# Layer norm without gain and bias in the stored rows: they come in with the turned copies and with GpSimd's residual rows

## The reference, cut to what matters

```python
def layer_norm(x, g, b):
    mu = mean(x); var = mean((x - mu) ** 2)
    return (x - mu) * rsqrt(var + 1e-5) * g + b

h = layer_norm(ALPHA * h + pool_mixer(h), ln_mix_g, ln_mix_b)     # ALPHA = 2 ** 0.25
gate, up = split(h @ w_gu)
f = (silu(gate) * up) @ w_down
out = layer_norm(ALPHA * h + f, ln_ffn_g, ln_ffn_b)
```

## Time and profile before

| | us |
|---|---|
| median of 3 runs | 1692.83 (1691.8 to 1693.13) |
| the profiled execution's own time | 1694.09 |
| its span, first to last instruction | 1692.3 |
| PE busy | 1660.9 (98%) |
| DVE busy | 977.0 (58%) |
| POOL busy | 608.9 (36%) |
| ACT busy | 582.9 (34%) |

### The profile page before, as it was taken

How to read it: one execution, slowest core, us unless ns; L and a number is a source line. 1 busy time by engine, 2 the same in 40 slices (tenths; PEclk the granted TensorE clock), 3 DMA queues, 4 the chain that set the end, 5 groups by cost and what they waited for, 6 DMA issues and landing times.

```text
span 1692.3 us, 19004 instructions
## 1 busy us (share of the span) xinstructions
PE 1660.9 (98%) x7400; PEld 1373.2 (81%) x7400; DVE 977.0 (58%) x1056; ACT 582.9 (34%) x790; POOL 608.9 (36%) x413
## 2 busy tenths in 40 slices
PE   7999999999999999999979999999999999999998
PEld 5888888788888888888868888888888888878886
DVE  6648677788744444444646554454554443558766
ACT  5322334244333333333533333333333332432220
POOL 0000015104445656465547666566532000341002
PEclk9999999999999999999999999999999999999999
DMA  8533647654354555465555555554659444554542
GB/s 316 207 125 128 242 143 282 244 211 168 114 173 156 187 193 193 143 223 173 185 172 181 162 159 163 173 152 137 196 143 336 151 135 155 191 196 174 197 156 92
DMA packets 182265, 305.66 MB, mean 181 GB/s; under 512 B 7584, under 2 KB 131616, under 8 KB 172448
## 3 DMA queue, kind: packets, MB, share of 16 engines
q1 hardware_dynamic: 142480, 272.46, 47.4%
q10 hardware_dynamic: 37520, 23.60, 4.6%
q0 software_dynamic: 2176, 8.39, 1.4%
HBM read 216.86 MB, written 87.56 MB: 180 GB/s over the span
## 4 chain that ended last, share of the span: by engine, by line
PE 92%; DVE 3%; DMA 3%; issue 1%; ACT 1%; SPq 0%; POOLq 0%; POOL 0%; DVEq 0%; ACTq 0%
PE acc L985 42%; PE acc L1014 18%; PE acc L831 9%; PE acc L847 9%; PE turn L985 7%; PE turn L1014 6%; PE turn L819 1%; DMA af_dram<-g 1%; DVE split L1342 1%; DMA z<-x 1%; DMA fold_dram<-fold_st 1%; DMA nat<-x_t 0%; DMA z<-w_group_t 0%; PE acc L892 0%; DVE sums L1375 0%
## 5 line engine op out<-in xcount | busy, mean ns | idle before, releaser
L985 PE MATMUL acc<-fb,wf 128*128 128x512 f32 x1584 | 364.5, 390 | 9.2 <-DVE g L1611 9.2
L985 PE MATMUL acc<-fa,wf 128*128 128x512 f32 x1584 | 366.1, 390 | 0.0
L985 PEld LDWEIGHTS acc<-fb,wf 128*128 128x128 f32 x1584 | 298.2, 188 | 71.7 <-issue 9.5
L985 PEld LDWEIGHTS acc<-fa,wf 128*128 128x128 f32 x1584 | 296.1, 188 | 61.2
L1014 PE MATMUL acc<-dw,da 128*128 128x512 f32 x1386 | 315.9, 389 | 0.7 <-DVE dw L1551 0.7
L1014 PEld LDWEIGHTS acc<-dw,da 128*128 128x128 f32 x1386 | 260.0, 188 | 55.5 <-DVE dw L1551 1.6
L1482 DVE TENSOR_TENSOR wf<-wt,wf 128x512 fp32r<-128x512 f32 x132 | 125.3, 950 | 180.8 <-ACT wf L1156 180.6
L1482 DVE TENSOR_TENSOR wf<-wr,wf 128x512 fp32r<-128x512 f32 x176 | 176.2, 1009 | 82.6 <-ACT wf L1156 82.1
L1156 ACT CAST wf<-wr 128x512 fp32r<-128x512 f32 x176 | 109.0, 620 | 236.1 <-PE acc L985 220.3
L681 POOL TENSOR_TENSOR wt<-wr,wt 128x512 f32<-128x512 f32 x88 | 129.4, 1471 | 147.4 <-DVE wf L1482 147.1
L847 PE MATMUL acc<-split,act_sb 128*128 128x512 f32 x768 | 176.7, 390 | 2.3 <-DVE split L1342 2.3
(11 more groups left out here) (108 smaller groups left out, 1634.3 us busy)
## 6 DMA issues: line engine op xcount, KB each, us to landing
wr<-w_gu SPq DMA_DIRECT2D x44, 1024.0 KB, 4.9
dar<-af_dram SPq DMA_DIRECT2D x56, 704.0 KB, 4.3
af_dram<-g ACTq DMA_DIRECT2D x33, 512.0 KB, 3.8
raw<-w_in SPq DMA_DIRECT2D x16, 1024.0 KB, 6.2
raw<-fold_dram SPq DMA_DIRECT2D x16, 1024.0 KB, 5.8
fs<-hf_dram SPq DMA_DIRECT2D x14, 1024.0 KB, 6.0
dt_raw<-w_down SPq DMA_DIRECT2D x22, 512.0 KB, 6.4
wt_dram<-dt_t SPq DMA_DIRECT2D x22, 512.0 KB, 3.8
```

Of the source, the lines that this page charges most:

```text
L985: mm = nc.tensor.matmul(dst, wf[:, slot, a, k, :], fa[half][i][:, v, :, k, :], start=i < 2 and k == 0 and n3 == 0, stop=k == KC - 1 and n3 ...
```

## The change

- `apply` and its two DVE passes over each of 16 tiles are gone. POOL's `rstd_of` also makes mean * rstd and its negative, `shift` (two operations on 128x4), and a new ACT operation `norm` makes z * rstd + shift in one pass over a tile. Stored and turned rows are then normalized, without g and b.
- `take_turn` multiplies by g and adds b, which now lie one value per partition (`mix_g_sb`, `mix_b_sb`): two ACT operations of 128x256 in place of one copy of 128x512.
- The residual rows in the down stage get ALPHA*g and ALPHA*b from POOL: two operations of 128x1024 for each of 16 tiles (32 in all). ALPHA is multiplied into a broadcast pair `mgb` by one ACT operation of 128x2048; ACT's 16 multiplications by ALPHA are gone. `mgb` is loaded when the last unit's first product is done. SP issues it behind the activations of step 2 and ahead of the residual rows.
- `take(k)` of t = 0 now waits for the row with gain (`hz_ready`), not for its landing.
- Five buffers `hs` in place of two; the first five tiles are loaded at k = 14 to 18.
- The early broadcast load of g and b (two of 512 KB) is replaced by two of 4 KB.

The core of the diff:

```diff
             def rstd_of(s):
                 pool.wait_ge(var_ready, s + 1)
+                if s:
+                    pool.wait_ge(normed, s * TT)
                 nc.gpsimd.tensor_tensor(rstd[:, 0:TT], var_eps[:, 0:TT], minus_half[:], ALU.pow).then_inc(rstd_ready, 1)
+                pool.wait_ge(rstd_ready, s + 1)
+                nc.gpsimd.tensor_tensor(mean_rstd[:], mv[:, 0:TT, 0], rstd[:, 0:TT], ALU.mult).then_inc(mean_scaled, 1)
+                pool.wait_ge(mean_scaled, s + 1)
+                sub(shift[:], zeros[:], mean_rstd[:]).then_inc(shift_ready, 1)
...
+            def rows_times_gain(rows, gained, ready, m):
+                nc.gpsimd.tensor_tensor(rows, rows, mgb[:, 0, :], ALU.mult).then_inc(gained, 1)
+                pool.wait_ge(gained, m + 1)
+                nc.gpsimd.tensor_tensor(rows, rows, mgb[:, 1, :], ALU.add).then_inc(ready, 1)
...
+            pool.wait_ge(mgb_scaled, 1)
+            for m in range(MT):
+                pool.wait_ge(hz_landed[m], 16)
+                rows_times_gain(z0[:, m].rearrange("p h t -> p (h t)"), hz_gained, hz_ready, m)
+            for m in range(len(hs)):
+                hs_times_gain(m)
             for m in range(MT):
                 pool.wait_ge(taken, taken_by(3, m))
-                pool.wait_ge(h12_scaled, m + 1)
+                pool.wait_ge(hz_ready, m + 1)
                 nc.gpsimd.tensor_tensor(z0[:, m, 1, :], z0[:, m, 1, :], z1[:, m, 1, :], ALU.add).then_inc(h12_added, 1)
-                pool.wait_ge(h2_scaled, m + 1)
+                pool.wait_ge(hs_ready, m + 1)
                 pool.wait_ge(h12_added, m + 1)
                 zz = z1[:, m].rearrange("p h t -> p (h t)")
-                nc.gpsimd.tensor_tensor(zz, zz, hs[:, m % 2], ALU.add).then_inc(h2_added, 1)
+                nc.gpsimd.tensor_tensor(zz, zz, hs[m % len(hs)][:], ALU.add).then_inc(h2_added, 1)
+                if m + len(hs) < MT:
+                    pool.wait_ge(h2_added, m + 1)
+                    hs_times_gain(m + len(hs))
...
-                nc.scalar.copy(st_of(pi)[:, :, k, :], turn[:, slot, :].rearrange("p (b t) -> p b t", t=P)
-                               ).then_inc(turn_taken, 1)
+                for n, kk in enumerate((k, KC + k)):
+                    nc.scalar.activation(st_of(pi)[:, 2 * n:2 * n + 2, k, :],
+                                         turn[:, slot, 2 * n * P:2 * (n + 1) * P].rearrange("p (b t) -> p b t", t=P),
+                                         ACT.Identity, bias=mix_b_sb[:, kk:kk + 1], scale=mix_g_sb[:, kk:kk + 1]
+                                         ).then_inc(turn_taken, 1)
...
+            def norm(s, j):
+                if j == 0:
+                    act.wait_ge(shift_ready, s + 1)
+                nc.scalar.activation(z[:, j, :], z[:, j, :], ACT.Identity, bias=shift[:, j:j + 1],
+                                     scale=rstd[:, j:j + 1]).then_inc(normed, 1)
...
             store_a(2 * JF - 1)
+            act.wait_ge(mgb_landed, 32)
+            nc.scalar.mul(mgb[:], mgb[:], ALPHA).then_inc(mgb_scaled, 1)
             for k in range(DSTEPS):
...
-                if t == 1:
-                    act.wait_ge(hz_landed[m], 16)
-                    nc.scalar.mul(z0[:, m, 1, :], z0[:, m, 1, :], ALPHA).then_inc(h12_scaled, 1)
-                if t == 3:
-                    act.wait_ge(hs_landed[m % 2], 16 * (m // 2 + 1))
-                    nc.scalar.mul(hs[:, m % 2], hs[:, m % 2], ALPHA).then_inc(h2_scaled, 1)
...
                 if t == 0:
-                    dve.wait_ge(hz_landed[m], 16)
-                    nc.vector.scalar_tensor_tensor(out=z0[:, m, 0, :], in0=z0[:, m, 0, :], scalar=ALPHA, in1=down_bank(k),
-                                                   op0=ALU.mult, op1=ALU.add).then_inc(taken, 1)
+                    dve.wait_ge(hz_ready, m + 1)
+                    nc.vector.tensor_tensor(z0[:, m, 0, :], z0[:, m, 0, :], down_bank(k), ALU.add).then_inc(taken, 1)
```

More of the change, by code:

```diff
@@ L131, in trunk @@
         dar = at("dar", V0, [P, 2, JF, P])
-        hs = at("hs", Z0, [P, 2, D])
+        hs = [at(f"hs{n}", off, [P, D]) for n, off in enumerate((Z0, Z0 + 4 * KB, G0, G0 + 4 * KB, G0 + 8 * KB))]
+        mgb = at("mgb", Z0 + 8 * KB, [P, 2, D])
         ident = sb("ident", [P, P])
         scale_sb = sb("scale_sb", [P, KT])
+        mix_g_sb = sb("mix_g_sb", [P, KT])
+        mix_b_sb = sb("mix_b_sb", [P, KT])
+        zeros = sb("zeros", [P, TT])
+        mean_rstd = sb("mean_rstd", [P, TT])
+        shift = sb("shift", [P, TT])
         stats = sb("stats", [P, 2 * MT, HALVES, 6])
@@ L169, in trunk @@
         hz_landed = [sem(f"hz_landed{m}") for m in range(MT)]
-        hs_landed = [sem("hs_landed0"), sem("hs_landed1")]
+        hs_landed = [sem(f"hs_landed{n}") for n in range(len(hs))]
+        mix_gb_landed = sem("mix_gb_landed")
+        mgb_landed = sem("mgb_landed")
         out_stored = sem("out_stored")
@@ L205, in trunk @@
         rstd_ready = sem("rstd_ready")
+        zeros_ready = sem("zeros_ready")
+        mean_scaled = sem("mean_scaled")
+        shift_ready = sem("shift_ready")
+        normed = sem("normed")
+        mgb_scaled = sem("mgb_scaled")
+        hz_gained = sem("hz_gained")
+        hz_ready = sem("hz_ready")
+        hs_gained = sem("hs_gained")
+        hs_ready = sem("hs_ready")
         centered = sem("centered")
@@ L519, in _ @@
             load_chunk(c_in(0, 1), 1, w_in[1])
-            for n, v in enumerate((mix_g, mix_b)):
-                sp.dma_start(gb[:, n, :], v.partition_broadcast(P)).then_inc(gb_landed, 16)
+            for tile, v in ((mix_g_sb, mix_gt), (mix_b_sb, mix_bt)):
+                sp.dma_start(tile[:], v).then_inc(mix_gb_landed, 16)
             load_chunk(c_in(0, 2), 0, w_in[2])
@@ L663, in _ @@
                         load_dw(t + 1, q)
[L664 to L667, removed]
+                if 14 <= k < 14 + len(hs):
+                    load_hs(k - 14)
+                if t == 3 and 3 <= m < 3 + MT - len(hs):
+                    load_hs(m - 3 + len(hs))
                 if t == 4 and 2 <= m < 2 + LATE:
@@ L1174, in mixer_block @@
                         take_turn(i - 1, 1)
+                    if b:
+                        for j in ((0, 1), (2,), (3,), ())[i]:
+                            norm(b - 1, j)
                     if b == LAST and i >= 2:
@@ L1274, in _ @@
                 nc.scalar.copy(s5[:], bank_d).then_inc(s5_taken, 1)
+                if n in (1, 2):
+                    norm(LAST, 2 * (n - 1))
+                    norm(LAST, 2 * (n - 1) + 1)
                 if turned_in(n)[0] is not None:
@@ L1407, in aggregate @@
             def aggregate(s):
+                if s:
+                    dve.wait_ge(normed, s * TT)
                 for j in range(TT):
@@ L1504, in mixer_block @@
                         d_lo(b, i - 1)
-                    if not first:
-                        for j in ((0, 1), (), (2,), (3,))[i]:
-                            apply(b - 1, j)
                     if b == LAST and i >= 2:
@@ L1591, in _ @@
                     up_out(jj, 0, bank(n, 0))
-                if n in (1, 2):
-                    apply(LAST, 2 * (n - 1))
                 if nxt:
@@ L1622, in _ @@
                     act_form_lo(1)
-                if n in (1, 2):
-                    apply(LAST, 2 * (n - 1) + 1)
                 if nxt:
```

61 lines of the change are left out of this document (32 added, 29 removed).

## The result

The median of the changed kernel is 1707.01 us (1704.1 to 1707.62, 4 runs), that of the kernel before in the same rounds 1692.93 us (1691.8 to 1693.13, 4 runs). The ratio is 1.0081 with a 95% interval of 1.0068 to 1.0093: slower by 14.1 us, where 14.6 were forecast. The profiled execution took 1707.62 us, its span is 1705.8 us at a mean granted clock of 0.992, 13.5 us over the span before. Of the later runs two single executions, 1860.45 us (run 6) and 6585.92 us (run 11), lie far outside all others, and no ratio counts them.

The account below looks back on a forecast made before the run. PE, busy 98% of the span with 31.4 us idle, was taken as the bound. Terms 0.4 + 10.2 + 4.0 = 14.6 us, added to the median 1692.83, gave 1707.4 us; range 1693 to 1717, likeliest case 1702 to 1717.

Parts of the forecast that it names:

- Hidden: Rival: POOL and DVE meet less, tile 6 is ready by 1320, only small terms stay; 1693 us, chance 0.13.
- Partly: Rival: part A of the down stage gives 4 to 8 us, C nothing; 1697 to 1702 us, chance 0.16.
- Table: Rival: Identity with bias makes ACT reload its table after each Silu, 0 to 20 us; chance 0.07 together with Worse.
- The parts that cost nothing: Removed DVE passes, norm, take_turn halves, early loads, dropped ACT multiplications: +0.4 us together, from take_turn (bounds 0 and 1.0).
- I take 0: Mixer: removing DVE's 32 passes (41 us) gains nothing, though worth at most 2.3 us of PE waits.
- Faster: Rival: without the DVE passes the mixer's waits, such as that at 309 us, shrink; 1689.4 us at best, chance 0.04.
- That wait ends with a DMA: Argument against Faster: the mixer wait at 309 us ends with a DMA; no size of its own.
- Part A: Down stage, t = 0: POOL's gains alternate with DVE's splits, so step 8 ends late: +10.2 us (bounds 0 and 14).
- Worse: Rival: PE standing repeatedly also loses clock, three or four times, above the upper bounds; 1717 to 1722 us, 0.07 with Table.
- Part B: Down stage, t = 1 and 2: five POOL pairs for hs fall on activation splits with 5 us in hand: 0, up to 1.
- Part C: Down stage, t = 3 to 4: POOL stays busy through the boundary, weight pieces wait: +4.0 us (bounds -0.75 and +9).
- Pieces 5 to 7 start 1.9 us earlier: Step in Part C: at the boundary these weight pieces start 1.9 us earlier, since ACT's multiplication is gone.

Follow-up runs that it names:

- run 6: Changed kernel with POOL's gains whole on hs tiles 0 to 4 only, 8 of 1024 columns on all other tiles: 1691.37 us.
- run 11: Second timing of the changed kernel with all 32 gain operations on DVE and mgb scaled after ACT's step 2 copy: 1691.11 us, ratio 0.9987.
- run 3: Changed kernel with each pair of POOL gain operations replaced by five memsets of the tile, which read nothing: 1694.56 us.
- run 1: Changed kernel with both POOL gain operations of every pair cut from 1024 to 8 columns, all waits and loads kept: 1691.06 us.
- run 12: Kernel with the gains on DVE, plus two spare DVE passes of 128x1024 for each of 12 mixer tiles: 1693.94 us.
- run 7: Changed kernel with ACT scaling mgb after its copy of the activations of step 2, not before: 1707.40 us.
- run 4: Changed kernel with POOL's gains whole on the z0 tiles only, 8 of 1024 columns on the hs tiles: 1697.19 us.
- run 8: Changed kernel with the reloads of hs tiles 5 to 7 issued on POOL's own DMA queue instead of by SP: 1702.15 us.
- run 9: Changed kernel with the hs reloads on POOL's own queue, hs gains whole, z0 gains on 8 columns: 1695.55 us.
- run 2: Changed kernel with POOL's gain operations cut to 512 of 1024 columns: 1693.66 us.

## Why the prediction was right, point by point

**The direction and the mechanism held.** POOL's gains hold DVE's splits and are held by them (3: without reads the holds and 12.5 us vanish); the rest of the change is free (1); the cost shows at the two product boundaries and nowhere else but for 0.7 us at step 2. The rivals *Hidden*, *Partly* and *Table* fell: there are still two table loads in the whole trace, none between Silus, with the new Identity copies among them:

```profile
L1123 ACT ACT_TABLE_LOAD x1 | 1.3, 1283 | 0.8 <-PEq L1821 0.8
...
L1279 ACT ACT_TABLE_LOAD x1 | 1.3, 1283 | 3.5 <-DVE fa L1528 3.5
```

By the Trainium skill, page "ScalarE: Activation LUTs", section "Table sets: the hidden batching unit", identity is in every set; the trace agrees, with that count.

**The sizes were right only in sum.** 14.6 against 14.1 came out of three errors that cancel, and that is luck. In the profile the parts are -3.0, +8.8 and +7.0, with +0.8 in the up stage that nobody forecast: 0.6 of it is clock, 24 matmuls behind the 9.0 us stop that took 7.73 us, not the 7.09 of the earlier trace rows.

- *The parts that cost nothing, sized +0.4: measured -3.0.* The step that failed is "I take 0" for DVE's passes, with the grown wait at 309 us. The *Faster* rival's mechanism, given a chance of 0.04, did take place, though it did not decide the sign. Before, POOL's last sum of turned rows in that place began at 289.27 and was held to 3.22 us by DVE's weight split, and DVE's x split was held to 2.31 in turn:

```profile
289.27 3.22 POOL L681 TENSOR_TENSOR ss_mix<-st_mix,ss_mix 128x512 f32<-128x512 f32 x1
291.27 2.31 DVE L1347 TENSOR_TENSOR mov<-nat,mov 128x1024 fp32r<-128x1024 f32 x1
...
301.93 0.69 DVE L1397 SCALAR_TENSOR_TENSOR z<-z,acc 128x512 f32<-128x512 f32 x1 [7.16 <-DMA z<-x]
```

  Now POOL's last sum begins at 285.94, ahead of both:

```profile
285.94 1.30 POOL L703 TENSOR_TENSOR ss_mix<-st_mix,ss_mix 128x512 f32<-128x512 f32 x1
...
291.25 1.22 DVE L1409 TENSOR_TENSOR mov<-nat,mov 128x1024 fp32r<-128x1024 f32 x1
...
298.83 0.69 DVE L1459 SCALAR_TENSOR_TENSOR z<-z,acc 128x512 f32<-128x512 f32 x1 [5.17 <-DMA z<-x]
```

  The x split ends 1.1 us earlier, SP issues the load of x rows behind it 1.1 us earlier, and they land 3.1 us earlier. "That wait ends with a DMA" was given as a reason against; a DMA is issued behind something, and that something had moved. Two halves cost 1.02 us against 0.59, as worked out; the longer copy mattered less than when it fell. How much of the 2.4 us in the mixer belongs to the removed passes is open: run 12 brought back 1.5 us, in other places than this one. The other 0.6 of the 3.0 lies ahead of the first chunk, whose start went from 37.2 to 39.3 us in the traces of kernels that do the same there, so it says nothing.

- *Part A, +10.2: the profile has +8.8, alone it is 6.1.* Two readings were too large. `mgb` lands 6.4 to 7.3 us after its issue, not 9.6, so step 2 stood 0.7 us and not 2.7; that this hardly touches the sum, as the forecast said, agrees with run 7. The period is 6.56 us, not 6.9: a multiplication held to 3.79, an addition held to 2.72. (The 6.9 does not come out of the forecast's own walk, which has 33.6 + 12.1 us for seven pairs, 6.5 each.) The first seven pairs took 43.9 us, not 45.7. With a stage that began 2.2 us earlier, tile 6 was ready at 1324.2, not 1328.0. The walk of the last pieces was right in kind: pieces 5 to 7 late by the holds, piece 10 by a load that waits for piece 7 (5.4 us from 1331.8 to its split, 5.5 forecast). The 6.1 of run 4 against 8.8 is in part one execution's luck: the same work cost 7.1 and 6.3 us at this place in the traces of runs 7 and 8, where PE waited 0.23 and 0.47 us for piece 10, not 1.25. In run 4 piece 10 was not waited for, and 3.2 of the 6.6 us that its rows show are the clock, which the forecast had only in the rival *Worse*.

- *Part B, 0: 0* (run 6).

- *Part C, +4.0: the profile has +7.0, alone it is 9.7.* It walked DVE's pieces through POOL's operations and found that part: 4.5 us by run 9 against run 1. The step that failed is "Pieces 5 to 7 start 1.9 us earlier": against the start of step 32 they started 3.2 us later than before. It missed a wait ahead of them. The change put the reload of tile 7 in SP's order, waiting for POOL to be done with the addition of tile 2; behind it in the same order stands the load of the activations of step 33, behind that (on ACT) the copies of pieces 5 to 10. Before, a reload with such a wait stood in that place too, but POOL was done in time. The prediction told of "a load of its own" for tiles 5 to 7 and did not ask who queues behind it on SP. Runs 8 and 9 put it at 5 us, the trace of run 8 at 3.9. The upper bound of +9 was short of the 9.7.

**The clock.** The rival *Worse* was to need such losses repeatedly. They came at each of the two boundaries: granted 0.86 and 0.93 in windows of 25 us, after stops of 0.7 to 1.8 us each that follow one another, and 12 matmuls at 0.45 us, the 1.2 GHz level, in place of 0.227. At step 8 they lay in front of a piece that was late anyway, which is why they cost little there. The sum had no term for the price of such stops, and it is not steady: see the last section.

## What to carry to other kernels

Two engines that each have room on the average can still not be filled side by side when their operations exclude each other: price the moved operation by what it does to the other engine's queue at the tightest boundary (here 32 operations of 2.4 us cost 16 us on POOL, and nothing that can be measured on the busier DVE, which does them in 1.22). When a load is put into an issue queue with a wait of its own, list everything that stands behind it in that queue; here that was some 5 us, a third of the loss. And a sum that comes out right is no proof of its terms: only the runs of one part alone showed three of them off by 3 to 6 us each.

## What the runs showed of the hardware

- POOL's memset of 128x1024 takes 0.95 to 0.96 us, and neither holds DVE's splits nor is held by them, in 4.95 us periods over eight tiles.
- DVE's take, which reads one operand from PSUM, is not held: 0.67 to 0.69 us each time, in the middle of POOL's operations of 3.8 us.
- The clock fell after two stops of 1.61 and 1.80 us, 0.96 us of matmuls apart, much shorter than the 9.0 us stop of the up stage, and some 14 matmuls went at half speed (run 4, granted 0.86 in 1325 to 1350 us). Stops of the same length need not do that: in run 2 stops of 0.30 and 1.80 us, in run 3 of 1.72 and 0.73 us, left the granted clock at 1.00 in 1500 to 1550 us.
- Half the columns in POOL's pairs cost 2.6 us, all of them 16.0.
